# Layer 0 mixer: gate scans, evictions and the gate's SiLU in other places; latent attention scores in head pairs

## What is computed

```python
def even_project(h, ...):
    q_g, k_g, v_g, r_g, lr_f, lr_b, c_q, c_kv, k_r = split(h @ w_in)
    gates  = log_sigmoid(lr @ wg2 + bg) / 16          # forward and backward, 4 heads x 64
    q  = (rms_norm(c_q, q_norm_g) @ w_uq)             # 4 heads x (128 plain + 64 rotary)
    kv = (rms_norm(c_kv, kv_norm_g) @ w_ukv)          # 4 heads x (128 key + 128 value)
def even_mixer(hc, hl, ...):
    # gated linear attention (GLA): decays are exp of running sums of the gates
    gla = rms_norm(o_forward + o_backward, norm_g) * silu(r_g)
    # latent attention (MLA): 4 heads, key = 128 plain + 64 rotary shared by the heads
    mla_l = softmax([q_l, rope(qr_l)] @ [k_all, rope(kr)].T / sqrt(192)) @ v_all   # 512 keys
    mla_c = softmax(q_c @ k_c.T / sqrt(192)) @ v_c                                   # 256 keys
    return concat([gla, mla]) @ w_out
```

## Time and profile before

| | us |
|---|---|
| runs, median (three: lowest, highest) | 2297.05 (2295.52, 2297.48) |
| the profiled execution, its own time | 2294.49 |
| its span from the first to the last instruction | 2292.7 |
| PE busy | 2215.0 |
| DVE busy | 1404.2 |
| ACT busy | 969.4 |
| POOL busy | 680.4 |

### The profile page before, as it was taken

The page is one execution under the profiler, slowest core; times in us unless marked ns, Lnnn a source line. Parts: engine busy times, 40 slices in busy tenths (PEclk is TensorE's granted clock), DMA queues, the critical chain, the costliest instruction groups (busy, mean ns, idle before and its releaser), DMA issues.

```text
span 2292.7 us, 33979 instructions
## 1 busy us (share of the span) xinstructions
PE 2215.0 (97%) x13172; PEld 1906.5 (83%) x13172; DVE 1404.2 (61%) x2117; ACT 969.4 (42%) x1571; POOL 680.4 (30%) x324
## 2 busy tenths in 40 slices
PE   8999999999999999989999999999999999989997
PEld 7989899988888877766788888878888878878997
DVE  4754554468887566666776766577655474446335
ACT  5665456543223255455532223253222254455443
POOL 3324245422222223311222222312222233223443
PEclk9999999999999999999999999999999999999999
DMA  8445545454454321210343543334544272223553
GB/s 282 150 166 222 220 155 197 164 194 182 176 219 180 104 96 58 84 37 19 110 140 144 189 159 109 106 140 152 187 183 165 92 149 91 74 73 131 175 180 105
DMA packets 79406, 329.98 MB, mean 144 GB/s; under 512 B 18912, under 2 KB 29280, under 8 KB 55696
## 3 DMA queue, kind: packets, MB, share of 16 engines
q1 hardware_dynamic: 79248, 327.81, 40.8%
HBM read 326.70 MB, written 1.08 MB: 143 GB/s over the span
## 4 chain that ended last, share of the span: by engine, by line
PE 86%; DVE 6%; ACT 4%; issue 3%; DMA 1%; POOL 1%; DVEq 0%; SPq 0%; ACTq 0%; POOLq 0%
PE ps L527 27%; PE ps L529 26%; PE ps L528 26%; PE ps L712 1%; DMA WF<-in_w 1%; PE ps L703 1%; ACT WH L1046 1%; PE ps L743 1%; PE ps L688 1%; PE ps L722 1%; DVE WL L1561 1%; POOL WL L2196 0%; DVE TMP L1664 0%; PE ps L674 0%; DVE AR L1973 0%
## 5 line engine op out<-in xcount | busy, mean ns | idle before, releaser
L2196 POOL TENSOR_TENSOR WL<-WF,WH 128x1024 fp32r<-128x1024 f32 (+2 forms) x252 | 593.4, 2355 | 1404.2 <-ACT WH L1046 1403.7
L527 PE MATMUL ps<-Hh,WH 128*128 128x256 f32 (+1 forms) x2536 | 859.5, 339 | 20.9 <-DVE WL L1561 7.1
L528 PE MATMUL ps<-Hl,WH 128*128 128x256 f32 (+1 forms) x2536 | 853.6, 337 | 0.0
L529 PE MATMUL ps<-Hh,WL 128*128 128x256 f32 (+1 forms) x2536 | 853.2, 336 | 0.0
L1046 ACT CAST WH<-WF 128x1024 fp32r<-128x1024 f32 (+3 forms) x506 | 465.2, 956 | 302.2 <-PE ps L529 293.1
L527 PEld LDWEIGHTS ps<-Hh,WH 128*128 128x128 f32 x2536 | 483.0, 190 | 82.7 <-issue 27.6
L529 PEld LDWEIGHTS ps<-Hh,WL 128*128 128x128 f32 x2536 | 483.0, 190 | 49.8
L528 PEld LDWEIGHTS ps<-Hl,WH 128*128 128x128 f32 x2536 | 483.2, 191 | 49.2 <-issue 0.5
L1637 DVE CUSTOM_DVE_ANT_0 TMP<-AR 128x1024 f32<-128x1024 f32 x216 | 398.3, 1883 | 11.4 <-DMA AR<-in_ada 10.4
L1561 DVE TENSOR_TENSOR WL<-WF,WH 128x1024 fp32r<-128x1024 f32 (+1 forms) x255 | 310.8, 1219 | 117.7 <-ACT WH L1046 116.6
L527 PE MATMUL ps<-HIDh,WH 128*128 128x512 f32 (+1 forms) x880 | 307.2, 349 | 3.7 <-DVE WL L1561 3.7
(11 more groups left out here) (230 smaller groups left out, 2021.5 us busy)
## 6 DMA issues: line engine op xcount, KB each, us to landing
WF<-in_w SPq DMA_DIRECT2D x170, 1024.0 KB, 4.8
AR<-in_ada SPq DMA_DIRECT2D x120, 512.0 KB, 5.7
WF<-in_w SPq DMA_DIRECT2D x80, 704.0 KB, 4.1
AR<-in_piece SPq DMA_DIRECT2D x12, 1024.0 KB, 8.3
AR<-bias_rows SPq DMA_DIRECT2D x3, 1024.0 KB, 13.1
AR<-in_rpb SPq DMA_DIRECT2D x12, 256.0 KB, 6.6
AR<-in_cond SPq DMA_DIRECT2D x2, 1024.0 KB, 7.0
X<-in_x SPq DMA_DIRECT2D x2, 512.0 KB, 4.5
```

The lines of the kernel that those rows point to most:

```text
L527: e.matmul(out, lh, rh, start=first, stop=False, skip_group_check=parts)
L528: e.matmul(out, lh, rl, start=False, stop=False, skip_group_check=parts)
L529: return e.matmul(out, ll, rh, start=False, stop=end, skip_group_check=parts)
L2196: e.tensor_tensor(l[:, k0:k1, :], src[:, k0:k1, :], h[:, k0:k1, :].bitcast(F32), ALU.subtract).then_inc(*up("p_lo", ("lo", i, 1)))
```

## The change

On DVE, the scans of the two n = 1 pairs leave the row of gates and go in front of the latents' scaling and behind level 5; `dve_decays(1)` comes after the low part of the next weight chunk; the low part of the chunk after uqr comes before level 7; the context copy of each rotary query tile (`qrc`) goes from ACT to DVE; DVE gives its two evictions of KN to ACT; and the item gnorms 0 goes from before the attention to behind the first row maximum. On ACT, the four Ln come directly behind the four Exp, ahead of the evictions of GK; the SiLU of r is made between the two last levels before ukv, for two of the four tiles straight from PSUM, which takes away their copies. On PE, the units of two heads run in turn, and their scores are made as a pair: both K = 128 products, then both rotary ones, on the two row halves. `work3` is written out as a list; it holds the items at the same iterations as before.

```diff
@@ -462,11 +462,11 @@
         })
 
     units3 = []
-    for h in range(4):
-        g = slice(64 * (h % 2), 64 * (h % 2) + 64)
+    for p in range(2):
         for r in range(2):
             k0, n = (0, T2) if r == 0 else (S, S)
-            for t in range(2):
+            for t, h in ((0, 2 * p), (0, 2 * p + 1), (1, 2 * p), (1, 2 * p + 1)):
+                g = slice(64 * (h % 2), 64 * (h % 2) + 64)
                 c = slice(S * r + P * t, S * r + P * t + P)
                 units3.append({
                     "s": [(0, n, [(QN[:, h, c], KN[:, h, k0:k0 + n]), (QR[g, h // 2, c], KR[g, k0:k0 + n])])],
@@ -492,7 +492,9 @@
     gla_items = [("level", i) for i in range(10)] + [("gouts", 0)] + [("level", i) for i in range(10, 13)] + [("gnorms", 0)]
     GLA_FIRST = len(gla_items)
     gla_items += [("level", i) for i in range(13, 20)] + [("gouts", 1), ("gnorms", 1)]
-    work3 = spread(gla_items[GLA_FIRST:], 16)
+    work3 = [[] for _ in range(19)]
+    for i, item in zip((1, 3, 5, 7, 9, 11, 13, 15, 16), gla_items[GLA_FIRST:]):
+        work3[i] = [item]
     GATES = [(0, 0), (1, 0), (0, 1), (1, 1)]
 
     units4 = []
@@ -761,10 +763,27 @@
                         pe_pieces(e, "y")
                     pe_stat(e, ("y", end // 4), S, [(HT[10], ("ysum", end // 4)), (HT[11 + end % 2], ("ysq", end))])
 
+    def pe_scores_rope(e, name, i, units):
+
+        b = []
+        for j in (i, i + 1):
+            b.append(ps.take(e, (name, "s", j), (name, "exp", j)))
+            for x in units[j]["sk"]:
+                e.wait_ge(*at(x))
+        for x in range(2):
+            c0, w, pairs = units[i + x]["s"][0]
+            e.matmul(b[x][:, c0:c0 + w], *pairs[0], start=True, stop=False)
+        for x in range(2):
+            c0, w, pairs = units[i + x]["s"][0]
+            e.matmul(b[x][:, c0:c0 + w], *pairs[1], start=False, stop=True).then_inc(*up("score", (name, "score", i + x)))
+
     def pe_attention(e, name, units, work, do):
         n = len(units)
         for i in range(n + 3):
-            if i < n:
+            if i < n and name == "mla":
+                if i % 2 == 0:
+                    pe_scores_rope(e, name, i, units)
+            elif i < n:
                 pe_scores(e, name, i, units[i])
             for item in work[i]:
                 do(e, *item)
@@ -1359,12 +1378,12 @@
         for i, (d, n) in enumerate(GATES):
             e.wait_ge(*at(("gabs", d, n)))
             e.activation(TMP[i], TMP[i], ACT.Exp, scale=-1.0).then_inc(*up("decay", ("gexp", d, n)))
+        for i, (d, n) in enumerate(GATES):
+            e.wait_ge(*at(("gexp", d, n)))
+            e.activation(TMP[i], TMP[i], ACT.Ln, bias=one).then_inc(*up("decay", ("gln", d, n)))
         act_splits(e, CH["e_k"][0])
         for j in range(2):
             act_evict(e, GK[:, j, :], ("gk", j)).then_inc(*up("a_evict", ("gk", j)))
-        for i, (d, n) in enumerate(GATES):
-            e.wait_ge(*at(("gexp", d, n)))
-            e.activation(TMP[i], TMP[i], ACT.Ln, bias=one).then_inc(*up("decay", ("gln", d, n)))
         for j in range(2):
             act_splits(e, CH["e_c"][j])
             some(1)
@@ -1391,24 +1410,24 @@
             act_evict(e, QN[:, j, :], ("qn", j)).then_inc(*up("a_evict", ("qn", j)))
         some(1)
         act_splits(e, CH["uqr"][0])
-        for j in range(2):
-            e.wait_ge(*at(("qrrot", j)))
-            e.copy(QR[:, j, con], ps["qr", j][:, con]).then_inc(*up("a_evict", ("qrc", j)))
         some(1)
         for j in range(2):
             act_splits(e, CH["e_r"][j])
             some(1)
-            for c in (2 * j, 2 * j + 1):
-                act_evict(e, GR[:, c, :], ("gr", c)).then_inc(*up("a_evict", ("gr", c)))
+            if j == 0:
+                for c in range(2):
+                    act_evict(e, GR[:, c, :], ("gr", c)).then_inc(*up("a_evict", ("gr", c)))
+            else:
+                act_silus(e)
+                for c in range(4):
+                    e.wait_ge(*at(("gr", c) if c < 2 else ("done", ("gr", c))))
+                    e.activation(GR[:, c, :], GR[:, c, :] if c < 2 else ps["gr", c], ACT.Silu).then_inc(
+                        *up("silu", ("grs", c), *([("gr", c)] if c >= 2 else [])))
             some(1)
         act_splits(e, CH["ukv"][0])
-        for j in (0, 2):
+        for j in range(4):
             act_evict(e, KN[:, j, :], ("kn", j)).then_inc(*up("a_evict", ("kn", j)))
         some(1)
-        act_silus(e)
-        for c in range(4):
-            e.wait_ge(*at(("gr", c)))
-            e.activation(GR[:, c, :], GR[:, c, :], ACT.Silu).then_inc(*up("silu", ("grs", c)))
         for t in range(4):
             act_evict(e, MV[:, t, :], ("mv", t)).then_inc(*up("a_evict", ("mv", t)))
         some(1)
@@ -2015,27 +2034,35 @@
             e.tensor_scalar(PF[:, d, n, :, 1:257], ps["gate", d, n].rearrange("p (s t) -> p s t", s=2), vec("bg_b" if d else "bg_f", n),
                             0.0, ALU.add, ALU.min).then_inc(*up("gate_min", ("gmin", d, n)))
         dve_splits(e, CH["e_k"][0])
-        for i, (d, n) in enumerate(GATES):
-            e.wait_ge(*at(("gln", d, n)))
-            e.wait_ge(*at(("gmin", d, n)))
-            e.tensor_tensor(PF[:, d, n, :, 1:257], PF[:, d, n, :, 1:257], TMP[i].rearrange("p (s t) -> p s t", s=2),
-                            ALU.subtract).then_inc(*up("gate_sub", ("gsub", d, n)))
+
+        def scan(d, n):
+
             for s in range(2):
                 e.memset(PF[:, d, n, s, 0:1], 0.0)
             e.wait_ge(*at(("gsub", d, n)))
             for s in range(2):
                 m = e.tensor_tensor_scan(PF[:, d, n, s, 1:257], view(one, 0, [0, S]), PF[:, d, n, s, 1:257], 0.0, ALU.mult, ALU.add)
             m.then_inc(*up("scan", ("pf", d, n)))
-            if i == 1:
-                dve_decays(e, 1)
+
+        for i, (d, n) in enumerate(GATES):
+            e.wait_ge(*at(("gln", d, n)))
+            e.wait_ge(*at(("gmin", d, n)))
+            e.tensor_tensor(PF[:, d, n, :, 1:257], PF[:, d, n, :, 1:257], TMP[i].rearrange("p (s t) -> p s t", s=2),
+                            ALU.subtract).then_inc(*up("gate_sub", ("gsub", d, n)))
+            if n == 0:
+                scan(d, n)
+        dve_splits(e, CH["e_c"][0])
+        dve_decays(e, 1)
         for j in range(2):
-            dve_splits(e, CH["e_c"][j])
+            if j:
+                dve_splits(e, CH["e_c"][j])
             some(1)
             dve_evict(e, CR[:, 2 * j + 1, :], ("c", 2 * j + 1))
         some(1)
         for i in range(2):
             dve_splits(e, CH["e_v"][i])
             some(1)
+            scan(*GATES[2 + i])
             if i == 0:
                 for k in range(4):
                     dve_scaled(e, CR[:, k, :], CR[:, k, :], vec("q_g", k) if k < 3 else vec("kv_g"), STAT[k // 3], ("cs", k), ("csq", k),
@@ -2047,25 +2074,25 @@
         e.wait_ge(*at(("cl", 3)))
         for j in (1, 3):
             dve_evict(e, QN[:, j, :], ("qn", j))
+        dve_splits(e, CH["uqr"][0])
         some(1)
-        dve_splits(e, CH["uqr"][0])
         for j in range(2):
             dve_rotate(e, QR[:, j, :], P, ps["qr", j], ("qr", j), STAT[j][:, 0:S], STAT[j][:, S:T2], ("qrrot", j), ("qr", j))
+            e.tensor_copy(QR[:, j, con], ps["qr", j][:, con]).then_inc(*up("d_evict", ("qrc", j)))
         some(1)
         for j in range(2):
             dve_splits(e, CH["e_r"][j])
             some(2)
         dve_splits(e, CH["ukv"][0])
-        for j in (1, 3):
-            dve_evict(e, KN[:, j, :], ("kn", j))
-        some(2)
+        some(1)
 
         def end(e, hr, b):
             h, r = hr
             c = slice(S * r, S * r + S)
             dve_low(e, Hl[:, h, c], b[:, 0:S], Hh[:, h, c], ("mlh", h, r), ("mll", h, r))
 
-        dve_attention(e, "mla", units3, 192 ** -0.5, work3, dve_gla, end)
+
+        dve_attention(e, "mla", units3, 192 ** -0.5, [gi + work3[0]] + work3[1:], dve_gla, end)
         for h in range(4):
             dve_low(e, Hl[:, 4 + h, :], GR[:, h, :], Hh[:, 4 + h, :], ("goh", h), ("gol", h))
         dve_mixer_out(e, "mix0", "eout", 0, T2)
```

## The result

The changed kernel takes 2301.5 us (median of 11 runs, 2296.58 to 2305.19), the kernel before, run beside it, 2297.05 (11 runs). The ratio is 1.0020, with a 95% interval of 1.0012 to 1.0028: 4.5 us **slower**, where 2295.5 was forecast and 2288.0 to 2299.5 given as the range. Its profiled execution took 2297.92 us, with a span of 2296.1; before it was 2294.49 and 2292.7.

A forecast was written before the change was run, and what follows sets the result against it. PE, busy 2215.0 of 2292.7 us, was taken as the bound. Terms 4.6 - 1.1 - 0.4 - 0.3 - 1.3 = 1.5 us turn the profiled 2294.49 into 2293.0; the median adds 2.56: 2295.5, range 2288.0 to 2299.5.

The forecast's parts named there:

- Term 1: Gates and e_c: PE's 3.12 us wait for a low part and 1.61 of half clock go, less 0.1: +4.6 us.
- Term 2: Latents' scaling: a pair of scans now ahead of it makes PE start level 5 later: -1.1 us.
- Term 3: Rotary queries and level 9: low part moved ahead, two context copies added on DVE: -0.4 us.
- Term 4: End of the projections: the 2.85 us key wait goes, but level 12 and the statistics come later: -0.3 us.
- Term 5: Attention: earlier start and overlapping rotary pairs, offset by unit order and waits before the last two pairs: -1.3 us.
- The half clock: Rival: gaps before the attention's last pairs pass 3 us, so pair and gouts run at half rate: 2302 us, chance 0.12.
- The lead survives: Rival: the attention keeps its early start, making term 5 +2.7 us and the time 2289.5 us; chance 0.29.
- The pair does not overlap: Rival: the paired rotary products in the attention do not overlap on PE: 2298 us, chance 0.07.

The follow-up runs named there:

- b3: The kernel before with the gates' and scans' edits alone: 2292.0 us, 0.16% faster.
- a1: The kernel before with the attention part of the change alone (new unit order, paired scores): 2303.88 us, 0.37% slower.
- d1: c1 with the rotary queries' edits undone (low part of uqr behind its level, context copies on ACT): 2289.78 us, ratio 0.9974.
- a3: The changed kernel with its new order of units kept, but scores made one unit at a time: 2291.53 us, 0.19% faster than before.
- a4: The changed kernel, but each pair takes its second unit's bank only after the first unit's plain product: 2292.87 us, 0.15% faster than before.
- b1: The changed kernel with two overwritten extra products between the takes of each pair's two banks, from unit 4 on: 2294.99 us, ratio 0.9995 to before.
- c1: a2 with the third pair of scans behind level 5's work instead of ahead of the latents' scaling: 2290.04 us, ratio 0.9977 to before.
- a2: The changed kernel without the attention part (units, levels' places and scores as before): 2288.85 us, 0.33% faster than before.
- b4: The kernel before with one DVE edit, the scaling of gnorms 0 behind the attention's first maximum: 2293.32 us, 0.14% faster.
- d2: d1 with five extra overwritten products of 256 columns ahead of the weighting of unit 14: 2287.38 us, 0.39% faster than before.
- c2: c1 with five extra products at level 9 and five between the weightings of units 14 and 15: 2294.08 us, ratio 0.9992 to before.
- c4: The changed kernel measured once more, unedited: 2299.01 us, 0.12% slower than before.

## Why the prediction was wrong

Its sum was +1.5 us. By the table, the profiled execution has -2.1 between gates and last weighting, -1.1 in eout, and -1.36 from before the gates, where the code is the same; +1.1 comes back later.

- **Term 1, +4.6: right, with some luck.** Gates to level 1 is 4.93 us shorter (b3 alone: 4.92). No low part is waited for. But the 0.1 for the evictions of GK holds only where the product before them, e_k, starts at half clock, as in the profile that was read. Where e_k runs at full rate, PE is through with it before ACT is through with the four Ln, and waits. PE at the start of e_c in a1, which has the old order on ACT, and in d1, which has the new one:

```profile
879.89 0.47 PE L529 MATMUL ps<-Hh,WH 128*128 128x512 f32 x1 [0.72 <-ACT AR L1101]
```

```profile
882.22 0.47 PE L527 MATMUL ps<-Hh,WH 128*128 128x512 f32 x1 [2.05 <-ACT AR L1082]
```

  Behind the 2.05 us some eight products run at half clock. So a3, a4, b1 and d1 have 30.88 in the first column for 29.5, and against a1's 32.88 the gain is 2.0 us and not 4.9.
- **Term 2, -1.1: right**, in size (-1.16) and cause: c1 takes the scan away from there and gets 1.17 back in that column.
- **Term 3, -0.4: sign right, size low.** It is -0.98. The step that failed is the hope that keys and POOL's product end together: POOL is done, and the keys behind two rotations, two copies and a low part end 0.95 us later.
- **Term 4, -0.3: 0.0.** The 2.85 us gap is gone, and 1.12 before level 12 and 1.74 before the statistics take its place: 2.86. ACT's new table load between SiLU and exp costs 1.28 us and no drain. ACT in a2:

```profile
988.72 1.28 ACT L1405 ACTIVATE AR<-ps 128x512 f32<-128x512 f32 x2 [6.09 <-PE ps L529]
990.02 1.28 ACT L1336 ACT_TABLE_LOAD   x1
991.31 1.06 ACT L1336 ACTIVATE AR<-AR 128x1024 f32<-128x1024 f32 x1
```

  The 2.66 us of the Trainium skill ("ScalarE: Activation LUTs", "What ACT_TABLE_LOAD costs") do not show here; only its load does.
- **Term 5, -1.3: wrong by 3.6**, and this is the failure. Its start was right: the first transposes come 2.96 us sooner behind the statistics in a2 (9.23 for 12.19) and 2.43 in the changed kernel, and the whole attention of a2 is 3.7 shorter. The order of units was put at 1.3 and costs 0.83. The overlap is there, 0.96 us for two rotary products of 512 keys (1003.59 to 1004.55) against 1.05 for one. What failed is the step "between the start and level 17 the pace is DVE's 7 us for two units, and PE's gain turns into waiting there". It took DVE's pace as given and counted the pair's wait only for the last two pairs. But the pair waits for the exp of unit i-1, the exp waits for DVE's maximum of i-1, and DVE's maximum of i waits for the pair. Taking both banks first closes that loop in every iteration, so six pairs wait 1.56 to 2.35 us, and DVE stands idle where it had set the pace. That is 4.2 us net of the overlap (b1). The waits forecast for the last two pairs came out right (2.4 us and 1.3, measured 2.35 and 1.56); the other four were not looked for. One reading behind this was wrong: "the exp of four units ago". With six takes for two units the bank comes back from two units ago. In the kernel before, unit 10's score waits for unit 8's exp (PE and ACT):

```profile
1041.94 0.70 PE L688 MATMUL ps<-HAh,AR 128*128 128x256 f32 x2 [0.18 <-ACT TMP L1100]
```

```profile
1041.11 0.69 ACT L1100 ACTIVATE TMP<-ps,SM 128x512 f32<-128x512 f32 x1 [2.56 <-DVE SM L1688]
```

  So there was one unit of slack to lose, and the pair takes it.
- **The half clock.** The rival had the mechanism and the time (2302 for 2301.5), but the wrong condition. "It decides from some 0.3 us more of wait" came from one row each of 2.85, 3.12 and 3.1 us. In other executions the 2.85 us gap is followed by half clock (b3, b4), 2.30 too, and 3.07 is not. Its 3.5 us stood mostly at the pairs of units 10 to 13, not at gouts. A chance of 0.12 was too low for a change that puts six new gaps of 1.5 to 2.5 us into a stretch that had few.
- *The lead survives* fell with the loop. *The pair does not overlap* fell too.

Left open: a1 and a2 add up to +0.9 us where the change costs 2.8 to 4.5. Some of that is the earlier start of the attention, worth 3.7 us with the old attention (a2) and 3.1 with the new (a1 against the changed kernel); the rest is no more than the intervals (2 to 3 us each) allow. And which gap meets half clock in an execution was not controlled by any run.

## What to carry to other kernels

Before two units are paired, write down for each bank which event of which earlier unit empties it, and follow that event back: if it leads through the engine that waits for the pair's own result, the pair takes a step of overlap out of the pipeline, whatever it saves on PE. Take each bank at the last moment (a4: 6 to 8 us for moving one line). And where PE waits some 2 us between dense stretches, products that are thrown away can be cheaper than the gap, but only inside the gap and shorter than it: b1 shows it, d2 points the same way within the noise, and c2 has them behind the gap and pays 3.7 us.

## What was not expected of the hardware

- **The granted clock behind one and the same gap differs between executions.** Level 9 behind 3.03 to 3.07 us took 2.00, 2.79 or 3.78 us; the pair of units 10 and 11 behind 2.30 and 2.33 us took 3.28 and 1.96; one values' product behind 2.84 to 2.86 us 0.50 or 0.80. One profile gives no threshold. The 3 to 9 us by which the runs of one kernel spread may come from it; no run shows that. The Trainium skill ("TensorE: Matmul & The Clock Gate", "Part 1: The HAM clock gate") says of a kernel's start that the count of slow matmuls varies between runs; these rows show it in mid kernel too, at 1.3 to 3 us a time, of which b3 gets its 1.45 back at the next wait for DVE.
- A gap of 2.15 us can be enough (d1, 3.51 us for 2.00). Behind single gaps of 1.6 us the pairs of the changed kernel ran at full rate, but the weighting that follows gaps of 1.14, 1.42 and 1.35 us close together ran at half (1.92 us for 1.06). In b1 and c4 the same three gaps were followed by full rate, so this too differs between executions. PE in the changed kernel:

```profile
1014.28 1.09 PE L714 MATMUL ps<-CST,TMP 128*128 128x128 f32 x4 [1.35 <-DVE TMP L1683]
1015.16 1.92 PE L724 MATMUL ps<-TMP,HAl 128*128 128x128 f32 x8
```

- Two fp32 products with K = 64 and 512 columns on different row halves take 0.96 us together (from 1003.59 to the next start), where one took 1.05. PE in the changed kernel:

```profile
1003.59 1.13 PE L778 MATMUL ps<-AR 64*128 64x512 f32 x4
1004.55 1.06 PE L894 MATMUL ps<-AR 64*128 64x128 f32 x16
```
